# One Trainium2 kernel: in the feed-forward stage, the order of a few helper steps at its first group border, which products are split, and how the residual is loaded back

## The reference

```
a = rmsnorm(x, norm2_g) @ w_up          # 1024 -> 2 x 2816, float32
a, state = causal_dwconv(a, buf, conv_w) # 3 taps
gate, up = split(a)
x = x + (silu(gate) * up) @ w_down      # 2816 -> 1024
```

## Time and profile before

| | us |
|---|---|
| median of 3 runs | 3309.49 |
| lowest and highest | 3307.84, 3313.08 |
| the profiled execution | 3305.48 |
| its span, first to last instruction | 3303.7 |
| TensorE busy in it | 3099.9 (94%) |
| VectorE | 2164.6 (66%) |
| ScalarE | 1279.6 (39%) |
| GpSimd | 1622.8 (49%) |
| mean granted TensorE clock | 0.965 |

### The profile page before, as it was taken

How to read it: one execution, slowest core, us unless ns; L and a number is a source line. 1 busy time by engine, 2 the same in 40 slices (tenths; PEclk the granted TensorE clock), 3 DMA queues, 4 the chain that set the end, 5 groups by cost and what they waited for, 6 DMA issues and landing times. The chain is left out here.

```text
span 3303.7 us, 60950 instructions
## 1 busy us (share of the span) xinstructions
PE 3099.9 (94%) x24810; PEld 2851.9 (86%) x24810; DVE 2164.6 (66%) x3139; ACT 1279.6 (39%) x2377; POOL 1622.8 (49%) x1196
## 2 busy tenths in 40 slices
PE   7999998899999999999989999979899999999996
PEld 5988875688999999999978898648799999998996
DVE  5396464564478877776666855535626887777666
ACT  4245144234434444433333441532425344444342
POOL 3222120114578988777442312002236798887873
PEclk8999998799999999999999999978999999999998
DMA  5733231202212222532265322330021122225322
GB/s 190 197 111 107 90 122 44 84 6 71 65 67 77 78 77 73 183 104 85 74 189 162 104 74 91 101 122 9 18 88 65 54 87 77 74 73 195 117 75 77
DMA packets 194974, 310.50 MB, mean 94 GB/s; under 512 B 38212, under 2 KB 125508, under 8 KB 191624
## 3 DMA queue, kind: packets, MB, share of 16 engines
q1 hardware_dynamic: 192616, 303.46, 28.0%
q10 hardware_dynamic: 2080, 3.15, 0.3%
HBM read 214.24 MB, written 89.82 MB: 92 GB/s over the span
## 5 line engine op out<-in xcount | busy, mean ns | idle before, releaser
L260 POOL TENSOR_TENSOR w_split<-w_full,w_split 128x1024 fp32r<-128x1024 f32 (+1 forms) x76 | 191.0, 2514 | 532.8 <-ACT w_split L252 532.8
L2601 PE MATMUL PS<-t_highs,block_high 128*128 128x288 f32 x1464 | 430.7, 294 | 1.5 <-DVE kept_sum_c L3165 1.5
L2605 PE MATMUL PS<-t_highs,block_low 128*128 128x288 f32 x1464 | 431.8, 295 | 0.0
L265 PE MATMUL PS<-h_split,w_split 128*128 128x384 f32 x1152 | 410.9, 357 | 21.1 <-PEq L198 10.0
L2603 PE MATMUL PS<-h_split,block_high 128*128 128x288 f32 x1452 | 428.0, 295 | 0.0
L267 PE MATMUL PS<-h_split,w_split 128*128 128x384 f32 x1152 | 390.9, 339 | 0.0
L266 PE MATMUL PS<-h_split,w_split 128*128 128x384 f32 x1152 | 389.9, 338 | 0.0
L2601 PE MATMUL PS<-h_split,block_high 128*128 128x288 f32 x1260 | 379.6, 301 | 3.3 <-ACT kept_sum_c L2840 3.1
L2605 PE MATMUL PS<-h_split,block_low 128*128 128x288 f32 x1260 | 371.3, 295 | 0.0
L2603 PE MATMUL PS<-x_lows,block_high 128*128 128x288 f32 x1104 | 325.1, 294 | 0.0
L2679 POOL TENSOR_TENSOR block_low<-block_sum,block_high 128x512 fp32r<-128x512 f32 (+1 forms) x212 | 297.8, 1413 | 1.6 <-ACT block_high L2803 1.5
(11 more groups left out here) (521 smaller groups left out, 8049.3 us busy)
## 6 DMA issues: line engine op xcount, KB each, us to landing
raw<-in_w_up SPq DMA_DIRECT2D x120, 256.0 KB, 2.9
act_keep<-ffn_up SPq DMA_DIRECT2D x44, 576.0 KB, 2.8
w_full<-in_w_in SPq DMA_DIRECT2D x40, 512.0 KB, 3.5
kq_keep<-split_rows SPq DMA_DIRECT2D x128, 128.0 KB, 2.4
kq_row<-kq_keep SPq DMA_DIRECT2D x32, 512.0 KB, 4.3
x<-x_keep SPq DMA_DIRECT2D x2, 4608.0 KB, 17.6
x_keep<-x SPq DMA_DIRECT2D x16, 576.0 KB, 5.5
raw<-in_w_down SPq DMA_DIRECT2D x48, 192.0 KB, 2.9
```

The source lines that it names most:

```text
L260: pool.tensor_tensor(ws[:, slot_of(n), 1, 0:w], wf[:, n % WSLOTS, 0:w], ws[:, slot_of(n), 0, 0:w].bitcast(F32), ALU.subtract).then_inc(w_l ...
L265: pe.matmul(out, w_hi, a_hi, start=first, stop=False)
L2601: pe.matmul(out[:, j], w_hi[i][:, w], moving(t, s, 0, k, cols), start=FRESH[i] and k == 0, stop=False, skip_group_check=True)
L2605: mm = pe.matmul(out[:, j], w_lo[i][:, w], moving(t, s, 0, k, cols), start=False, stop=k == inner(s) - 1, skip_group_check=True)
```

## The change

It does five things, in both layers.

1. Product A22 of pair 4 is split and no longer whole. T4's low part for the up pairs is made by VectorE at the end of pair 3 (it was at the start of pair 5) and by GpSimd in its pair 5 (it was 6).
2. S4 of pair 21 is split; pairs 25 and 29 have no whole product left (they had S3 and A22).
3. In the first pairs of the groups, low parts move on VectorE: B22's from behind `upper_left` of pair 24 and 28 to ahead of it, and from pair 21 to the end of pair 20; T3's to the end of pairs 24 and 28; T4's to the head of pairs 25 and 29 (it was 26 and 30).
4. In pair 20, T2's low part goes behind `upper_right` and `lower_right`. The two convolutions of the last up tile stand apart: the gate one at the end of pair 20, the up one in pair 21 behind its `lower_right`.
5. x is loaded back by row pairs (k, k + 4) and all 1152 columns, in the order of use, in place of quadrants of four rows by 576 columns.

```diff
@@ -2267,8 +2267,8 @@
             def x_out(s, p, j):
                 return x[:, (s - UPS) % HK + HK * p, HALF * j:HALF * (j + 1)]
 
-            WHOLE = {0: (S1, S2, S3, A22), 1: (S2, S3, A22), 2: (S3, A22), 3: (A22,), 4: (A22,)}
-            SECOND = ((S4, S3, A12, A22),) + ((S3, A22),) * (GROUPS - 1)
+            WHOLE = {0: (S1, S2, S3, A22), 1: (S2, S3, A22), 2: (S3, A22), 3: (A22,)}
+            SECOND = ((S3, A12, A22),) + ((),) * (GROUPS - 1)
             for g in range(GROUPS):
                 WHOLE[UPS + HK * g] = (A11, S1, S2, S4, S3, A12, A22)
                 WHOLE[UPS + HK * g + 1] = SECOND[g]
@@ -2326,7 +2326,6 @@
                 st12_in, st22_in, st21_in = many[25:28]
                 x_back, late_in, (lhigh, llow) = many[28:32], many[32:36], many[36:38]
                 r12, r22 = (r12a, r12b), (r22a, r22b)
-                X_BACK = ((0, 1), (1, 1), (0, 0), (1, 0))
                 DOWN = LATE // 2
 
                 def down_unit(c, u):
@@ -2404,9 +2403,9 @@
                         sp.dma_start(late_raw[i][:, :], act_keep[:, FF_TILES - LATE + i, :]).then_inc(late_in[i], 16)
 
                     def load_x(i):
-                        p, j = X_BACK[i]
-                        ks, cols = slice(HK * p, HK * (p + 1)), slice(HALF * j, HALF * (j + 1))
-                        sp.dma_start(x[:, ks, cols], x_keep[:, ks, cols]).then_inc(x_back[i], 16)
+                        rows = "p (e k) c -> p e k c"
+                        sp.dma_start(x[:, :, :].rearrange(rows, e=2)[:, :, i, :],
+                                     x_keep.rearrange(rows, e=2)[:, :, i, :]).then_inc(x_back[i], 16)
 
                     sp.dma_start(old[:, :, :], d["c_fconv"][l]).then_inc(aux, 16)
                     g_lo, g_hi = PC["norm1_g"]
@@ -2570,7 +2569,7 @@
                             else:
                                 pe.wait_ge(blo, split_no[s, i])
                                 if s < UPS:
-                                    if t < B11 and s == t + 1 + (t == T4):
+                                    if t < B11 and s == t + 1:
                                         pe.wait_ge(rdy[t], 2)
                                 elif (s - UPS) % HK in (1, 2):
                                     pe.wait_ge(rdy[t], (s - UPS) // HK + (3 if t < B11 else 1))
@@ -2724,7 +2723,7 @@
                         ins.then_inc(rdy[B11], 1)
 
                     def low_of_sum(t):
-                        pool.wait_ge(pdn, 7 * (t + (t == T4)) + MOVING.index(t) + 1)
+                        pool.wait_ge(pdn, 7 * t + MOVING.index(t) + 1)
                         pool.wait_ge(chi[t], 1)
                         if t == T2:
                             pool.wait_ge(csum[T4], 1)
@@ -2737,7 +2736,7 @@
                         first, second = (BORDERS.index(s - i) if s - i in BORDERS else None for i in (1, 2))
                         low_of(s, A11)
                         sum_of(s, S1)
-                        if s == 6:
+                        if s == 5:
                             low_of_sum(T4)
                         if s <= UPS:
                             taps_ahead(2 * (s + 1))
@@ -3174,7 +3173,7 @@
 
                     def add_kept(s, p, j, n):
                         if s < UPS + HK:
-                            dve.wait_ge(x_back[X_BACK.index((p, j))], 16)
+                            dve.wait_ge(x_back[s - UPS], 16)
                         xs = x_out(s, p, j)
                         dve.tensor_tensor(xs, xs, kept[n][:, :], ALU.add).then_inc(kev, 1)
 
@@ -3212,7 +3211,7 @@
                                               ALU.mult).then_inc(ev, 1)
                         else:
                             if s < UPS + HK:
-                                dve.wait_ge(x_back[X_BACK.index((1, 0))], 16)
+                                dve.wait_ge(x_back[s - UPS], 16)
                             xs = halves(x_out(s, 1, 0))
                             dve.tensor_tensor(xs, xs, banks(s, "x"), ALU.add).then_inc(ev, 1)
 
@@ -3240,8 +3239,6 @@
                     finish(1)
                     for s in range(UPS - 1):
                         f = s + PLAIN
-                        if s == 5:
-                            low_of_sum(T4, 4)
                         upper_right(s)
                         lower_right(s)
                         if s < 3:
@@ -3251,6 +3248,8 @@
                         next(taps)
                         lower_left(s)
                         next(taps)
+                        if s == 3:
+                            low_of_sum(T4, 3)
                         finish(f)
                     s = UPS - 1
                     upper_right(s)
@@ -3262,20 +3261,20 @@
                     s = UPS
                     low_of_sum(T1, s)
                     t4_sum(0)
-                    low_of_sum(T2, s)
                     upper_right(s)
                     lower_right(s)
+                    low_of_sum(T2, s)
                     upper_left(s)
                     lower_left(s)
+                    low_of_rows(0)
                     convolve(FF_TILES - 1, 0)
-                    convolve(FF_TILES - 1, 1)
                     for s in range(UPS + 1, PAIRS):
                         g = BORDERS.index(s) if s in BORDERS else None
                         step = (s - UPS) % HK
                         if step == 0:
                             low_of_sum(T1, s)
                             low_of_sum(T2, s)
-                        if step == 2:
+                        if s - 1 == last_whole((s - 1 - UPS) // HK, A22):
                             low_of_sum(T4, s - 1)
                         if s == PAIRS - 1:
                             dve.wait_ge(lhigh, 1)
@@ -3284,17 +3283,20 @@
                         upper_right(s)
                         lower_right(s)
                         if s == UPS + 1:
+                            convolve(FF_TILES - 1, 1)
                             product(FF_TILES - 1)
                         if g is not None:
                             t1_sum(g)
+                        if s == last_whole((s - UPS) // HK, S4) and s > UPS + 1:
+                            low_of_rows((s - UPS) // HK)
                         upper_left(s)
                         if g is not None:
                             t2_sum(g)
-                        if s == last_whole((s - UPS) // HK, S4):
-                            low_of_rows((s - UPS) // HK)
-                        if step == 1:
+                        if s == UPS + 1:
                             low_of_sum(T3, s)
                         lower_left(s)
+                        if step == 0:
+                            low_of_sum(T3, s)
                         if g is not None:
                             t3_sum(g)
                             t4_sum(g)
```

## The result

| | before | after |
|---|---|---|
| median | 3312.18 us (14 runs) | 3318.72 us (14 runs) |
| lowest and highest | 3307.12, 3320.73 | 3312.05, 3327.57 |
| profiled execution, its span | 3305.48, 3303.7 | 3312.05, 3310.0 |

The ratio is 1.0020, 95% interval 1.0012 to 1.0029: slower by 6.5 us. The forecast was 3308 in a range from 3295 to 3315.

A forecast was written before the change was run, and what follows sets the result against it. TensorE, busy 94% of the span, was taken as the bound. Gains of 15.1 us against 9.8 of new waits and 3.9 of clock gave -1.4 us on 3305.48, carried over to 3308; range 3295 to 3315.

The forecast's parts named there:

- Pairs 25 and 29, the wait before S2: Pairs 25, 29: S2 waits about 3.3 us for ScalarE's copy behind S3's cast; four such pairs cost 9.8 us.
- The turns written there: From 1472.2, VectorE and GpSimd alternating by instruction: S3's sum ends at 1481.65 in place of 1479.93.
- What comes behind in pair 26: After S2's wait: B21's low part ends about 1490.3 against 1491.0, A22's about 1491.4 against 1493.3.
- The clock: Pairs 25, 29: half clock behind four gaps of 3.3 us costs 3.9 us, between one and two drops.
- +9.7 forecast for these pairs: Pairs 24 to 26 and 28 to 30, both layers together: forecast change in length of +9.7 us.
- First border, what is late next: Pairs 20 to 22: T2's, B22's, S4's low parts and kept_sum_a have little slack; 0.6 us a layer given back.
- the prediction's own signs of being wrong: S2's gap in pair 25 below 2 us, clock drops at none or all gaps, or pair 21 or 22 gap over 1.
- Pair 20: Last product's 3.00 us wait closes with T2's low part behind the joins: gain 4.8 us, plus 2.8 for layer 1's clock.
- Up pairs: Pairs 3 to 6: pair 5's wait for kept_sum_c goes; gain 1.1 us after giving back 0.2 us a layer.
- Rival A: Pairs 25, 29: S2 waits 1.5 us or less, no clock drop; 3297 us; chance 0.33.
- Rival B: Pairs 25, 29: every 3.3 us gap brings half clock, low parts of B21 and A22 late; 3319 us; chance 0.15.

The follow-up runs named there:

- e5: Changed kernel, with ScalarE in pairs 25, 26, 29, 30 copying product 0 before that pair's casts and product 1 before the next A11's; 3313.44 us, 1.0003 of before.
- e1: Changed kernel with pairs 25 and 29 as before (S3, A22 whole; low parts of B22, T3, T4 in old places); 3302.94 us, 0.9976 of before.
- e11: e1, with ScalarE copying product 0 of pair 23 before that pair's casts and product 1 before the next A11's; 3305.05 us, 0.9980 of before.
- e9: Kernel before with only the late groups' part: no whole product in pairs 25, 29, low parts of B22, T3, T4 moved; 3330.98 us, 1.0053 of before.
- e2: Changed kernel with x loaded back in quadrants as before; 3318.43 us, 1.0019 of before.
- e4: Changed kernel with B22's low part of pairs 24 and 28 behind the upper-left join and add again; 3314.60 us, 1.0014 of before.
- e10: e1 with S4 of pair 21 whole again and B22's low part of group 0 back in pair 21; 3308.43 us, 0.9988 of before.
- e8: Changed kernel with A22 of pairs 25, 29 whole again, B22's low part behind upper-left, T4's in pairs 26, 30; 3317.55 us, 1.0015 of before.

## Why the prediction was wrong, by its steps

- **Pairs 25 and 29, the wait before S2.** The mechanism was right and the size in total: "about 3.3 us" before S2, where 2.05 to 2.35 stand before S2 and pair 24 is 1.1 longer; the sum's end was right within 0.1 us. The turns written there add up only with two pieces of B11's low part of 1.26 each ahead of the sums. The second of them then ends at 1472.2 + 1.26 + 1.85 + 1.26 = 1476.6, 21.2 us after the start of pair 24, and TensorE wants it at 20.15. The prediction never held the two against each other. That moved 1.1 us without adding to it.
- **What comes behind in pair 26** is the step that failed there. The prediction looked at the low parts of B21 and A22 for slack and not at the copy of kept_sum_a, which stands behind the casts of pair 26 and so behind its last sum. It costs 1.5 us (pair 26 takes 18.23, where 16.67 is an all-split pair) where TensorE has kept the full clock. e5 shows that even without it GpSimd is late, for B21.
- **The clock.** "I take 3.9", for four gaps. In two of the four stretches the clock fell, but the stretches are as long as the others. Windows over the first products behind the gap, full clock in layer 0 and fallen in layer 1 (columns as in the earlier trace rows):

```profile
1485.55:1489.60 4.05, 4.05 (x31) 4.05 (x32) 0.57 (x1) 1.70 (x3) 4.05 (x4) 1.00 0.29 84
3108.41:3112.40 3.99, 3.99 (x19) 3.99 (x20) 0.57 (x1) 1.05 (x2) 3.99 (x4) 0.57 0.29 87
```

  Pair 25 takes 19.04 us in layer 0 and 20.57 in layer 1, pair 26 takes 18.23 and 16.67: the 1.5 us that the slow clock takes in pair 25 is taken off the wait in pair 26, since GpSimd goes on meanwhile. So in each of the four stretches one or the other costs 1.5 us, some 6 in all, where the prediction had 3.9 for the clock and nothing for pair 26. That the one error nearly pays for the other is luck: +9.7 forecast for these pairs, +11.2 measured.
- **First border, what is late next.** "I give back 0.6 a layer" for pairs 21 to 23 was 1.6 and 1.9 in fact (length +1.1 and +1.4 where 0.5 was to be saved). The list named kept_sum_a at 1422.6 against 1423.1; in the trace VectorE needs 4.25 us for the taps where the trace of before has 3.54 for them, and S2 waits 0.6 to 1.4 us for ScalarE's copy. A gap over 1 us in pair 22 was one of the prediction's own signs of being wrong, and layer 0 has it (1.43). And pair 23 was not on the list: counted from the start of pair 20, TensorE begins pair 23 in layer 0 of e1 2.5 us earlier than before and GpSimd's last sum for it ends only 1.2 earlier, and the copy stands behind that sum's cast there too. e11 shows it by taking the wait away.
- **Pair 20.** 1.48 us of the gap are left in layer 0 of the profiled execution and none in layer 1. The ten kernels with the new order give twenty cases: in this one pair 20 took 21.87, in the others 20.15 to 20.62. The length goes with T4's second load: landing within 5.66 us of its issue gives 20.15 or 20.16 (but for the 20.41 of layer 1 of after, where x was late), 5.73 to 6.48 gives 20.41 to 20.62, the one of 6.72 gives 21.87. The reading of the step was right; that the load scatters was not in it.
- **Up pairs.** The wait before A22 of pair 5 went as forecast, one of 0.80 before S4, for ScalarE's copy of kept_sum_c, came in its place in both layers. It makes the pair 1.0 us longer, where "I give back 0.2 us a layer" was allowed.
- Rival A, the likeliest by chance (0.33), had the wait in pair 25 at its low end. It is out. In after and e9 the sum ended where the turns put it in all eight stretches, and where it ended early (one stretch each of e2, e4 and e5) the time was lost behind A12 of pair 29. Rival B came nearest by its number (3319), and that is luck: its grounds, a drop in every gap and A12 and A22 of pair 25 late, are not what after shows.

The sum failed by 6.5 us in the loops: 1.1 in the up pairs, 1.6 in pair 20 (landing of a load), 2.3 in pairs 21 to 23, 1.5 in the late pairs. From 3308 to the measured 3318.7 it is 10.7 us. Of the rest, 1.5 lies outside the loops and is open, and 2.7 is the level: 3309.49 was the median of three runs of the kernel before, 3312.18 is that of 14.

## What to carry to other kernels

When a faster engine or an earlier need is forecast, hold every in-order helper's copy and cast of the next two stages against the new times, not only the operands of the product at hand: ScalarE's copies stand behind casts that hang on GpSimd. A split that saves 0.5 us on the bound engine must find helpers with room, and the low part that comes with it must find a place. In the first group a split, with B22's low part moved into pair 20, was worth 2.1 to 2.2 us a layer (e1 against e10); in the second and third the splits of S3 and A22, with the low parts moved as they need, cost 2.7 to 3.0 us a stretch. Undo a change that has several parts part by part before judging it: here the new order at the first border was a gain (pair 20 in e1 3.3 and 5.6 us shorter than before, pairs 21 to 23 only 1.7 and 1.4 longer) and the splits of the two later groups a loss, and with those taken out the kernel takes 0.9976 of the time before instead of 1.0020.

## What the runs showed of the hardware

- VectorE and GpSimd take turns by whole instructions when both work from SBUF on two inputs: a chain of nine instructions played through by turns hit the end of the ninth within 0.1 us (26.3 us after the start of pair 24 forecast, 26.2 measured). It is no strict rule: at 1463.65 us of after GpSimd's low part for A11 takes 3.36 us, since VectorE does two instructions in a row (1464.14 to 1466.16) before GpSimd has its turn. VectorE's joins, which read one input from PSUM, keep their 0.74 us beside GpSimd.
- A drop of the granted clock right behind a gap need not cost anything, if another engine is the bound at the next wait: in after and e9, stretches with the drop take 58.47 to 58.77 us and without it 58.53. Where no such wait follows it costs its full 1.5 us: 58.07 against 56.54 in e8, 58.53 against 57.01 in e5.
- Gaps of one length are followed by the half clock or not: 2.05 us at 1485.55 and 2.07 at 3108.41 of after (granted clock 1.00 and 0.57), 2.07 and 2.06 in e8 (0.58 and 1.00), 3.00 twice in before (1.00 and 0.50).
- A load of 288 KB issued just ahead of four of 1152 KB landed 4.6 to 6.7 us after its issue (4.9 to 6.3 with quadrants, 4.6 to 6.7 with row pairs), and in the new order the length of pair 20 scattered from 20.15 to 21.87 us with it.
